# Expert weights of a hybrid decoder layer: tiles as single 1 MB transfers of one matrix, and what follows for the matmuls

## The reference

```
lg = (xt @ wg) + bg
grp = argmax(lg)                       # 4 groups, one per token
le_g = the 8 expert logits of the token's group
top_p, top_i = top_k(softmax(le_g), 2)
w = p_grp * top_p / sum(top_p)         # combine[t, e] from w, 32 experts in all
h = silu(einsum('td,edf->tef', xt, w_gate)) * einsum('td,edf->tef', xt, w_up)
h = h * combine[..., None]
y = einsum('tef,efd->td', h, w_down)   # D = 2048, expert width F = 256
```

## Time and profile before

| | |
|---|---|
| median of 3 runs | 1046.58 us (1046.55 to 1047.31) |
| span of the profiled execution | 1042.4 us (the median lies 4.2 us above it) |
| TensorE busy | 1007.5 us, 97% |
| VectorE busy | 745.5 us, 72% |
| ScalarE busy | 601.9 us, 58% |
| mean DMA rate | 260 GB/s over the span |

### The profile page before, as it was taken

The page is one execution under the profiler, slowest core; times in us unless marked ns, Lnnn a source line. Parts: engine busy times, 40 slices in busy tenths (PEclk is TensorE's granted clock), DMA queues, the critical chain, the costliest instruction groups (busy, mean ns, idle before and its releaser), DMA issues.

```text
span 1042.4 us, 13131 instructions
## 1 busy us (share of the span) xinstructions
PE 1007.5 (97%) x4610; PEld 820.7 (79%) x4610; DVE 745.5 (72%) x647; ACT 601.9 (58%) x562; POOL 5.4 (1%) x21
## 2 busy tenths in 40 slices
PE   5999999998999998999999999999999999999995
PEld 5788888887777787888889788889788889788883
DVE  4654444678666555788884988885988885988884
ACT  6543434338565335577774677764676764677771
POOL 1000000000000000000000000000000000000000
PEclk9999999999999998999999999999999999999999
DMA  9955555555533551599995899995899994899972
GB/s 305 340 204 165 198 165 197 162 162 203 173 110 113 194 160 60 184 360 370 372 368 199 283 357 375 366 367 185 292 365 366 369 369 176 301 362 374 370 279 82
DMA packets 98072, 271.07 MB, mean 260 GB/s; under 512 B 11044, under 2 KB 20856, under 8 KB 97912
## 3 DMA queue, kind: packets, MB, share of 16 engines
q1 hardware_dynamic: 97904, 270.60, 72.9%
q10 hardware_dynamic: 136, 0.04, 0.0%
HBM read 268.51 MB, written 2.10 MB: 260 GB/s over the span
## 4 chain that ended last, share of the span: by engine, by line
PE 92%; DVE 3%; ACT 3%; DMA 1%; issue 0%; SPq 0%; DVEq 0%; ACTq 0%
PE ps L1246 26%; PE ps L1248 26%; PE ps L1247 26%; PE ps L1521 5%; DVE w_lo L708 1%; ACT w_hi L382 1%; PE ps L1343 1%; PE ps L1538 1%; PE ps L1372 1%; PE ps L1552 1%; PE ps L1479 1%; PE ps L1270 1%; PE ps L1539 1%; ACT xT_hi L391 1%; DMA x<-in_x 1%; PE ps L1358 0%
## 5 line engine op out<-in xcount | busy, mean ns | idle before, releaser
L708 DVE TENSOR_TENSOR w_lo<-raw,w_hi 128x2048 fp32r<-128x2048 f32 x251 | 574.1, 2292 | 171.1 <-ACT w_hi L382 170.2
L382 ACT ACTIVATE w_hi<-raw 128x2048 fp32r<-128x2048 f32 x251 | 480.7, 1918 | 201.8 <-PE ps L1248 198.8
L1246 PE MATMUL ps<-w_hi,xg_hi 128*128 128x512 f32 x512 | 205.3, 401 | 0.0
L1247 PE MATMUL ps<-w_lo,xg_hi 128*128 128x512 f32 x512 | 202.3, 395 | 0.0
L1248 PE MATMUL ps<-w_hi,xg_lo 128*128 128x512 f32 x512 | 202.2, 395 | 0.0
L1246 PE MATMUL ps<-w_hi,xT_hi 128*128 128x512 f32 x288 | 115.1, 400 | 2.8 <-DVE w_lo L726 2.6
L1248 PEld LDWEIGHTS ps<-w_hi,xg_lo 128*128 128x128 f32 x512 | 96.0, 187 | 23.6
L1247 PE MATMUL ps<-w_lo,xT_hi 128*128 128x512 f32 x288 | 114.4, 397 | 0.0
L1248 PE MATMUL ps<-w_hi,xT_lo 128*128 128x512 f32 x288 | 114.3, 397 | 0.0
L1246 PEld LDWEIGHTS ps<-w_hi,xg_hi 128*128 128x128 f32 x512 | 96.4, 188 | 21.8
L1247 PEld LDWEIGHTS ps<-w_lo,xg_hi 128*128 128x128 f32 x512 | 96.2, 188 | 21.7
(11 more groups left out here) (235 smaller groups left out, 846.3 us busy)
## 6 DMA issues: line engine op xcount, KB each, us to landing
raw<-in_exp_w_gate SPq DMA_DIRECT2D x128, 512.0 KB, 5.0
raw<-in_exp_w_up SPq DMA_DIRECT2D x128, 512.0 KB, 6.3
raw<-in_exp_w_down SPq DMA_DIRECT2D x128, 512.0 KB, 5.5
raw<-in_w_in SPq DMA_DIRECT2D x36, 1024.0 KB, 5.1
raw<-in_w_out SPq DMA_DIRECT2D x16, 1024.0 KB, 5.3
raw<-in_cmp_w_k SPq DMA_DIRECT2D x4, 1024.0 KB, 6.7
raw<-in_cmp_w_v SPq DMA_DIRECT2D x4, 1024.0 KB, 5.4
x<-in_x SPq DMA_DIRECT2D x4, 512.0 KB, 6.2
```

What stands on the lines that cost most here:

```text
L382: act.activation(w_hi[:, slot, :], raw[:, rslot, :], ACT.Copy).then_inc(hi_ready, 1)
L708: dve.tensor_tensor(w_lo[:, slot, :], raw[:, rslot, :], w_hi[:, slot, :].bitcast(F32), ALU.subtract).then_inc(lo_ready, 1)
L1246: pe.matmul(dst, l_hi, r_hi, start=start, stop=False, skip_group_check=True)
L1247: pe.matmul(dst, l_hi, r_lo, start=False, stop=False, skip_group_check=True)
```

## The change

A tile becomes a single transfer of 1 MB, 8 KB for each partition, of one matrix. Tiles 0 and 1 of an expert are the two halves of gate's rows, tiles 2 and 3 those of up. `gate_up` therefore has 24 matmuls of 256 columns for a tile, and the gate half of the PSUM bank is complete after the second tile. A down tile is one half f of the hidden width over all 2048 columns, so that all four output banks are open until the last down tile. A new semaphore `y_half` tells ScalarE that banks 0 and 1 are complete in the middle of that tile.

In the first expert of group 0 TensorE now issues the gathers 0, 1 and 2, then tile 0 (which needs parts 0 and 1), then gather 3, and waits for all four parts ahead of tile 1. ScalarE and VectorE evacuate parts 2 and 3 one after the other, behind tile 3 and ahead of tile 4. In the last group the scatters no longer stand between the two halves of the last down tile.

```diff
--- before.py
+++ after.py
...
@@ -211,9 +212,7 @@

             if kind == "rows":
                 return t.rearrange("p (c n) -> p c n", c=4)
-            if kind == "gu":
-                return t.rearrange("p (w c n) -> p w c n", w=2, c=4)
-            return t.rearrange("p (f n) -> p f n", f=2)
+            return t.rearrange("p (c n) -> p c n", c=8)

         w_in_v = w_in.rearrange("(p c) n -> p c n", c=KC)
         w1_v = [w.rearrange("l d e -> d l e") for w in (cmp_w1_k, cmp_w1_v)]
@@ -286,15 +285,13 @@

             def load_gu(e, n, slot, c):
                 slot_free(n)
-                dst = tile_views(raw[:, slot, :], "gu")
-                sp.dma_start(dst[:, 0], gate_v[e, :, 4 * c:4 * c + 4, :]).then_inc(raw_in[slot], 16)
-                sp.dma_start(dst[:, 1], up_v[e, :, 4 * c:4 * c + 4, :]).then_inc(raw_in[slot], 16)
-
-            def load_down(e, n, slot, half):
+                dst = tile_views(raw[:, slot, :], "half")
+                src = gate_v if c < 2 else up_v
+                sp.dma_start(dst, src[e, :, 8 * (c % 2):8 * (c % 2) + 8, :]).then_inc(raw_in[slot], 16)
+
+            def load_down(e, n, slot, f):
                 slot_free(n)
-                dst = tile_views(raw[:, slot, :], "down")
-                for f in range(2):
-                    sp.dma_start(dst[:, f, :], down_v[e, :, f, 1024 * half:1024 * half + 1024]).then_inc(raw_in[slot], 16)
+                sp.dma_start(raw[:, slot, :], down_v[e, :, f, :]).then_inc(raw_in[slot], 16)

             def group_loads(q, grp):
                 n0 = first_of(q)
...
@@ -601,7 +598,7 @@
             def ring_hi(q):

                 def at(p):
-                    hi(first_of(q) + p, slot=p % SPL, rslot=p % RAW, count=160 + 32 * EPG * q + 32 * (p // RAW + 1))
+                    hi(first_of(q) + p, slot=p % SPL, rslot=p % RAW, count=160 + 16 * EPG * q + 16 * (p // RAW + 1))
                 return at

             def gathered(q, r):
@@ -627,8 +624,8 @@
                     router_exps()
                 at(3)
                 gathered(q, 2)
+                gathered(q, 3)
                 at(4)
-                gathered(q, 3)
                 at(5)
                 silu(q, 0, 3)
                 hT_evac(q, 0)
...
@@ -667,8 +664,10 @@
                     hT_evac(q, EPG - 1)
                     at(47)
                 for nb in range(4):
-                    if nb % 2 == 0:
-                        act.wait_ge(tile_used, n0 + PER_GRP - 1 + nb // 2)
+                    if nb == 0:
+                        act.wait_ge(y_half, q + 1)
+                    if nb == 2:
+                        act.wait_ge(tile_used, n0 + PER_GRP)
                     act.activation(yg_hi[:, 512 * nb:512 * nb + 512], ps[:, nb, :], ACT.Copy).then_inc(yghi_ready, 1)
                 if into_next:
                     for p in range(51, 54):
@@ -1540,10 +1539,12 @@

             def gate_up(n, place, c4):
                 pe.wait_ge(lo_ready, n + 1)
-                r_hi, r_lo = (tile_views(w[:, place % SPL, :], "gu") for w in (w_hi, w_lo))
-                for c in range(4):
-                    ins = split3(ps[:, 4, :], xg_hi[:, 4 * c4 + c, :], xg_lo[:, 4 * c4 + c, :], r_hi[:, :, c, :],
-                                 r_lo[:, :, c, :], start=(c4 == 0 and c == 0), stop=(c4 == 3 and c == 3))
+                r_hi, r_lo = (tile_views(w[:, place % SPL, :], "half") for w in (w_hi, w_lo))
+                dst = ps[:, 4, F * (c4 // 2):F * (c4 // 2) + F]
+                for c in range(8):
+                    k = 8 * (c4 % 2) + c
+                    ins = split3(dst, xg_hi[:, k, :], xg_lo[:, k, :], r_hi[:, c, :], r_lo[:, c, :],
+                                 start=(k == 0), stop=(k == KC - 1))
                 used(ins)

             def hidden_T(q, e):
@@ -1552,16 +1553,16 @@
                     ins = pe.transpose(ps[:, 7, P * f:P * f + P], hval[:, f::2], ident[:, :])
                 ins.then_inc(hT_done, 1)

-            def down(n, place, half, start=False, ks=range(2)):
+            def down(n, place, f, start=False, last=False):
                 pe.wait_ge(lo_ready, n + 1)
-                r_hi, r_lo = (tile_views(w[:, place % SPL, :], "down") for w in (w_hi, w_lo))
-                for k in ks:
-                    for f in range(2):
-                        ins = split3(ps[:, 2 * half + k, :], hT_hi[:, f, :], hT_lo[:, f, :],
-                                     r_hi[:, f, 512 * k:512 * k + 512], r_lo[:, f, 512 * k:512 * k + 512],
-                                     start=start and f == 0, stop=False)
-                if 1 in ks:
-                    used(ins)
+                r_hi, r_lo = w_hi[:, place % SPL, :], w_lo[:, place % SPL, :]
+                for k in range(4):
+                    cs = slice(512 * k, 512 * k + 512)
+                    ins = split3(ps[:, k, :], hT_hi[:, f, :], hT_lo[:, f, :], r_hi[:, cs], r_lo[:, cs],
+                                 start=start and f == 0, stop=False)
+                    if last and k == 1:
+                        ins.then_inc(y_half, 1)
+                used(ins)

             def second_expert(q, n0):

@@ -1576,11 +1577,13 @@
             def first_expert(q):
                 n0 = first_of(q)
                 pe.wait_ge(sel_ready, q + 1)
-                gather(q, 0)
-                for c4 in range(4):
-                    if c4 < 3:
-                        gather(q, c4 + 1)
-                    pe.wait_ge(xglo_ready, 4 * q + c4 + 1)
+                for r in range(3):
+                    gather(q, r)
+                pe.wait_ge(xglo_ready, 4 * q + 2)
+                gate_up(n0, 0, 0)
+                gather(q, 3)
+                pe.wait_ge(xglo_ready, 4 * q + 4)
+                for c4 in range(1, 4):
                     gate_up(n0 + c4, c4, c4)
                 pe.wait_ge(cmb_ready, 1)
                 take_shares(q)
@@ -1621,7 +1624,7 @@
                 down(n0 + 46, 4, 0)
                 pe.wait_ge(selT_ready, q + 1)
                 if into_next:
-                    down(n0 + 47, 5, 1)
+                    down(n0 + 47, 5, 1, last=True)
                     pe.wait_ge(xglo_ready, 4 * q + 8)
                     gate_up(n0 + 48, 0, 0)
                     gate_up(n0 + 49, 1, 1)
@@ -1640,11 +1643,8 @@
                     transpose_sel()
                     second_expert(q + 1, n0 + PER_GRP)
                 else:
-                    down(n0 + 47, 5, 1, ks=(0,))
-                    for k in range(4):
-                        scatter(q, k)
-                    down(n0 + 47, 5, 1, ks=(1,))
-                    for k in range(4, 8):
+                    down(n0 + 47, 5, 1, last=True)
+                    for k in range(8):
                         scatter(q, k)
                     pe.wait_ge(scat_added, 8 * q + 8)

```

More of the change, by code:

```diff
@@ L577, in _ @@
                 m = T_OUT + 8 + 2 * b
-                hi(m + 3, count=None if m + 3 < T_MOE else 160 + 32)
+                hi(m + 3, count=None if m + 3 < T_MOE else 160 + 16)
                 if b:
@@ L581, in _ @@
                 if b < 3:
-                    hi(m + 4, count=None if m + 4 < T_MOE else 160 + 32)
+                    hi(m + 4, count=None if m + 4 < T_MOE else 160 + 16)
                     squares(b)
@@ L593, in _ @@
                 act.activation(hn[:, t, :], hn[:, t, :], ACT.Copy, scale=st[:, 58 + t:59 + t]).then_inc(hn_ready, 1)
-            hi(T_MOE + LEAD - 1, count=160 + 32)
+            hi(T_MOE + LEAD - 1, count=160 + 16)
             def router_exps():
@@ L645, in other_experts @@
                         hi(n0 + 6 * j - 2 + c, slot=(1 + c) % SPL, rslot=(4 + c) % RAW,
[L646 removed]
+                           count=160 + 16 * EPG * q + 16 * (j if c < 2 else j + 1))
                         if c == 1:
```

2 lines of the change are left out of this document (1 added, 1 removed).

## The result

The changed kernel takes 1053.9 us (median of 4 runs, 1053.16 to 1054.27) where the kernel before takes 1046.57 (4 runs): a ratio of 1.0077, 95% interval 1.0057 to 1.0096. It is slower by 7.3 us; the forecast was 1052.0, 5.4 us slower.

The account below looks back on a forecast made before the run. The prediction took TensorE's instruction cost as the bound, with transfers hidden. Gate/up 1.5, down 0, transfers 0, first expert 3.5 and end 0.4 gave +5.4 us, 1052.0 us; the likeliest case (73%) ranged from 1049 to 1061.

Parts of the forecast that it names:

- Gate and up, +1.5 us: Gate/up tiles: 1536 matmuls of 512 columns become 3072 of 256, at 1 ns more per pair, +1.5 us.
- the compression row: Compression-stage matmuls, 256 columns over a 30-column stationary tile, 0.1164 us apart; as gate/up's price, -0.8 us.
- the attention row: Attention's full-precision matmuls over a full stationary tile: two of 256 cost 2.5 ns more than one of 512, +3.8 us.
- Both bounds: Limits for the gate/up term: -0.8 us from the compression stage and +10.3 us from the gate projection.
- Weight loads: Gate/up's doubled 128-column loads: 0.111 us each, just fitting behind a 256-column matmul with some 5 ns to spare.
- Down and transfers, 0: Down tiles keep 12 matmuls of 512 columns; larger expert transfers stay hidden under TensorE's work: 0 us each.
- First expert, +3.5 us: Group 0's first expert: TensorE waits for the last xg_lo, hidden transposes start 3.5 us later; bounds 2.3 and 4.5.
- Tile 1 then runs to 428.8: First expert's second tile: starts at 426.0 us after the last xg_lo and ends at 428.8.
- End, +0.4 us: Last group's end: the first half is ready only within the last down tile, +0.4 us (0 to 1.5).
- The weight load as the pace: Gate/up rival: loads can't run wholly beside the short matmuls, spacing over 0.1167 us, most likely 1091 us; chance 6%.
- a matmul faster than in proportion: Gate/up rival: 256-column spacing falls toward 0.108 us, -22.7 us in all, 1023.9 us; chance 8%.
- Nothing to measure: Whole-kernel rival: compression-stage spacing and a partly absorbed first-expert delay, +1.9 us, 1048.5 us, within 0.2%; chance 13%.

Follow-up runs that it names:

- experiment 5: Kernel before with only down tiles as halves of the rows, `y_half` and the new order at the end: 1045.37 us against 1046.19, ratio 1.0006.
- experiment 4: Changed kernel with each expert tile brought by two transfers of 512 KB instead of one: 1052.86 us, ratio 1.0076 to the kernel before.
- experiment 9: Changed kernel with two unused matmuls ahead of each of TensorE's two first-expert waits: 1049.96 us against 1054.28 unfilled; ratio 1.004 to the kernel before.
- experiment 3: Changed kernel with tiles interleaved gate, up, gate, up, so the last two gathered parts are awaited ahead of tile 2: 1048.51 us, ratio 1.0033 to the kernel before.
- experiment 7: Changed kernel with five unused matmuls ahead of tile 1's wait, longer than that wait: 1054.75 us against 1046.19 for the kernel before, ratio 1.0088.
- experiment 2: Kernel before with only the first expert's new order of gathers, tile 0 and evacuations: 1051.98 us against 1045.28, ratio 1.0058.
- run 8: Kernel before with four and three unused matmuls in two router waits, product with up moved earlier, last wait inside the branch: 1046.54 us against 1046.19, ratio 1.0008.
- run 10: Kernel before with two and one unused matmuls in two router waits, product with up moved earlier, last wait inside the branch: 1044.03 us against 1045.17, ratio 0.9989.
- run 11: Changed kernel with tiles interleaved, two VectorE moves, two and one unused router-wait matmuls, last wait inside the branch: 1046.09 us against 1045.17 before, ratio 1.0002.

## Why the prediction was right, and where it was not

- **What bounds the kernel: right.** TensorE is busy 559.07 of 560 us between 450 and 1010 us, after as before.
- **Gate and up, +1.5 us: right, 1.3.** The pair costs 0.84 ns more, next to the 1 ns chosen between the compression row and the attention row. Both bounds held and the upper one, from the gate projection, was far off. The Trainium skill, page "TensorE: Matmul & The Clock Gate", section "Back-to-back issue gap", gives a fixed part of about 2.5 ns for each matmul, by which the doubled count would cost an estimated 3.8 us; the trace doesn't agree for these operands, it shows a third of that (0.84 ns more for a pair).
- **Weight loads: right.** A load of 128 columns lies in each distance of 0.117 us. The rule in the Trainium skill, same page, section "The mechanism", that a load overlaps a running matmul only where the row groups differ, is contradicted here, since all loads and matmuls use all 128 rows and a pair one after the other would take 0.228 us. The same section of the Trainium skill also lets a load for the background weight buffer run ahead; the trace doesn't speak against that.
- **Down and transfers, 0: right** (experiments 5 and 4). The DMA share fell as forecast and nothing came of it.
- **First expert, +3.5 us: chain right, one term mis-sized; measured +6.1.** The waits came as worked out: 2.1 us ahead of tile 1 (2.3 forecast), on the chain gather, tile 0, copy of tile 3, `lo`, last `xg_lo`. The step that failed is "Tile 1 then runs to 428.8". It took tile 1 as 2.8 us. Behind the idle time TensorE ran at clock 0.50 and the tile took 5.3 us. Everything that follows is late by that: with the 2.13 us shift of this profile the prediction puts the end of tile 1 at 430.9, the next `lo` at 433.1, the one behind the shares at 437.0 and the transposes at 440.0; they came at 433.5, 435.72, 439.66 and 442.60, 2.6 late each. So the delay lies above the upper bound of 4.5 us, and of the signs named for a right forecast one failed: the transposes came 6.1 us late and not 3 to 4. With the idle time filled, the first expert's delay is 3.75 us (experiment 9), near the 3.5 forecast. I had read the granted clock of the windows and never asked what a new idle time of 2 us does to it.
- **End, +0.4 us: right for the chain, 0.3 in experiment 5;** 1.3 in the profile of the kernel after, where the clock fell behind the 1.44 us wait and the second half took 5.3 us (1040.84 to 1046.16) in place of 4.4.
- **Rivals.** The weight load as the pace, and a matmul faster than in proportion, are ruled out by 0.117 us. "Nothing to measure" is ruled out by the interval. The transfer had no part.

With the clock left out the sum is 1.3 + 3.75 + 0.3 = 5.4 us, the forecast; 4.8 us by the medians (1049.96 less 1045.17) and 4.2 by the ratio was measured where the waits are filled. The 1.9 us that the forecast lacks are the clock behind the first expert's wait, 2.4 to 2.6 us by the profiles. Why filling the waits recovered 4.3 us, 1.9 more than the first expert accounts for, stays open; a profile is of one execution, and the dips elsewhere (+2.1 us ahead of the first gather in this one, absent in some others) differ between executions.

## What to carry to other kernels

Price a new wait on TensorE with what follows it: here a wait of 2.1 us cost another 2.5 us, because the tile behind it ran at a granted clock of 0.50. Price a stretch at the low clock with what runs in it: tile 1 took 5.3 us in place of 2.8, the gathers no longer than before. Before tiles are recut, list which inputs each new tile needs and when they become ready. Here a single-matrix tile needed all the gathers one tile earlier, and ordering the tiles gate, up, gate, up with two moves on VectorE left no loss that the runs could show. A work that only occupies the engine can tell the cost of a wait from that of the clock, but size it from the row of the very instruction and check that the clock is still up ahead of it.

## What the runs showed of the hardware

- The granted clock fell to 0.50 behind waits of TensorE of 2.1 to 2.4 us, in most but not all cases: in the kernel after behind the first such wait and not behind the second (in both of its profiles), in experiments 3 and 7 behind the second, in experiments 2 and 4 behind both. Behind the same wait of 1.84 us it stayed up in the kernel before and fell in experiment 5 (1.85). Behind waits of 0.99 and 1.44 us it fell in some executions. What decides it stays open.
- At that level a 256-column float32r matmul comes every 0.213 us (0.117 at full clock). The instructions of the gathers, 128 full-precision columns with a weight load each, come every 0.219 us (0.218 at full clock), so the low clock costs them next to nothing.
- A full-precision matmul of 512 columns is two instructions, 0.43 us each at full clock.
- The span ends with TensorE's branch over code that isn't run: from the last addition to the end of the span 5.2 to 7.0 us, and 4.1 to 4.6 in runs 8, 10 and 11, where its last wait stands inside the branch.
